# One sum row per token in DRAM instead of four expert rows, in a hybrid decoder layer with 32 experts on Trainium2

## What is computed

```python
x = x + concat([o_da, o_rw]) @ w_out
h = rmsnorm(x, ffn_norm_w)
x = x + moe_ffn(h, ...)          # top 4 of 32 experts per token
return rmsnorm(x, final_norm_w)

# in moe_ffn, per expert block of rows:
gu = xb @ mlp1_w[e] + mlp1_b[e]
act = (up + 1.0) * gate * sigmoid(1.702 * gate)      # clamped gate and up
y = (act @ mlp2_w[e] + mlp2_b[e]) * row_gate
out = zeros((T + 1, D)).at[row_tok].add(y)[:T]
```

## Time and profile before

| | us |
|---|---|
| median of three runs | 1646.55 |
| the three runs | 1646.4, 1647.76, 1646.55 |
| the profiled execution | 1647.25 |
| its span, first to last instruction | 1645.4 |
| TensorE busy | 1574.4 (96%) |
| VectorE busy | 1347.0 (82%) |
| ScalarE busy | 1069.3 (65%) |
| GpSimd busy | 320.8 (19%) |

### The profile page before, as it was taken

The page is one execution under the profiler, slowest core; times in us unless marked ns, Lnnn a source line. Parts: engine busy times, 40 slices in busy tenths (PEclk is TensorE's granted clock), DMA queues, the critical chain, the costliest instruction groups (busy, mean ns, idle before and its releaser), DMA issues.

```text
span 1645.4 us, 28008 instructions
## 1 busy us (share of the span) xinstructions
PE 1574.4 (96%) x10337; PEld 1271.1 (77%) x10338; DVE 1347.0 (82%) x1188; ACT 1069.3 (65%) x1011; POOL 320.8 (19%) x223
## 2 busy tenths in 40 slices
PE   5999999987899999999999999999999999999994
PEld 4677777765778888888888888888888888888883
DVE  5556565556489999999999999999999999999984
ACT  4534343434367777777777777777777777777772
POOL 6300000000102212222121222312222232212222
PEclk9999999998899999999999999999999999999997
DMA  6611111006299999999999999999999999999899
GB/s 194 248 49 32 49 32 47 2 2 221 105 389 350 384 354 367 356 369 357 373 376 361 377 356 365 371 367 360 366 360 348 366 366 362 365 366 366 348 323 210
DMA packets 100718, 467.26 MB, mean 284 GB/s; under 512 B 12696, under 2 KB 39352, under 8 KB 51377
## 3 DMA queue, kind: packets, MB, share of 16 engines
q1 hardware_dynamic: 86032, 429.65, 68.7%
q0 software_dynamic: 14624, 36.74, 7.2%
HBM read 454.84 MB, written 28.31 MB: 294 GB/s over the span
## 4 chain that ended last, share of the span: by engine, by line
PE 71%; DMA 3%; DVE 1%; issue 1%; ACT 0%; PEld 0%; POOL 0%; DVEq 0%; ACTq 0%; POOLq 0%; PEldq 0%
PE psum L1888 29%; PE psum L1891 14%; PE psum L1916 13%; PE psum L1921 6%; PE psum L1294 3%; DMA x<-expert_rows 2%; PE psum L1878 2%; PE psum L1868 2%; PE psum L1904 1%; PE psum L1858 1%; DMA xg<-h_rows,gath_i 0%; DVE w_pieces_lo L1697 0%; PE psum L1310 0%; ACT w_pieces_hi L1562 0%; PE psum L1302 0%
## 5 line engine op out<-in xcount | busy, mean ns | idle before, releaser
L1697 DVE TENSOR_TENSOR w_pieces_lo<-w_pieces,w_pieces_hi 128x2048 fp32r<-128x2048 f32 x384 | 871.0, 2288 | 78.4 <-ACT w_pieces_hi L1562 78.4
L1562 ACT ACTIVATE w_pieces_hi<-w_pieces 128x2048 fp32r<-128x2048 f32 x384 | 736.4, 1919 | 279.3 <-PE psum L1891 204.9
L1888 PE MATMUL psum<-w_pieces_hi,xh 128*128 128x512 f32 x1024 | 292.4, 407 | 0.5 <-DVE xl L1708 0.5
L1888 PE MATMUL psum<-w_pieces_hi,xl 128*128 128x512 f32 x1024 | 276.0, 391 | 0.0
L1891 PE MATMUL psum<-w_pieces_lo,xh 128*128 128x512 f32 x1024 | 275.7, 391 | 0.0
L1888 PEld LDWEIGHTS psum<-w_pieces_hi,xl 128*128 128x128 f32 x1024 | 192.8, 188 | 43.1
L1891 PEld LDWEIGHTS psum<-w_pieces_lo,xh 128*128 128x128 f32 x1024 | 192.3, 188 | 42.7
L1888 PEld LDWEIGHTS psum<-w_pieces_hi,xh 128*128 128x128 f32 x1024 | 181.7, 190 | 41.8 <-issue 11.8
L1516 POOL DMA_INDIRECT expert_rows<-ys,this_i x30 | 158.8, 5294 | 246.5 <-issue 246.5
L1916 PE MATMUL psum<-w_pieces_hi,ah 128*128 128x512 f32 x512 | 160.8, 395 | 0.0
L1916 PE MATMUL psum<-w_pieces_hi,al 128*128 128x512 f32 x512 | 158.2, 390 | 0.0
(11 more groups left out here) (363 smaller groups left out, 1938.7 us busy)
## 6 DMA issues: line engine op xcount, KB each, us to landing
w_pieces<-in_mlp_w SPq DMA_DIRECT2D x384, 1024.0 KB, 6.9
w_raw<-in_w_in SPq DMA_DIRECT2D x26, 512.0 KB, 4.0
expert_rows<-o_t POOLq DMA_DIRECT2D x4, 2048.0 KB, 14.3
x<-expert_rows POOLq DMA_DIRECT2D x16, 512.0 KB, 9.4
w_pieces<-in_w_out SPq DMA_DIRECT2D x8, 512.0 KB, 9.2
chunk_work<-in_x SPq DMA_DIRECT2D x4, 512.0 KB, 5.9
x<-in_x SPq DMA_DIRECT2D x4, 512.0 KB, 13.7
h_rows<-w_pieces POOLq DMA_DIRECT2D x4, 512.0 KB, 3.0
```

Of the source, the lines that this page charges most:

```text
L1562: nc.scalar.activation(hi[:, p % RING], raw[:, raw_slot(b, p)].rearrange("p r n -> p (r n)"), ACT.Copy).then_inc(s_hi, 1)
L1697: nc.vector.tensor_tensor(lo[:, p % RING], raw[:, raw_slot(b, p)].rearrange("p r n -> p (r n)"), hi[:, p % RING].bitcast(F32), ALU.subtrac ...
L1888: nc.tensor.matmul(bank(up_bank(b) + c), a[:, k, :], hi[:, p % RING, c * 512:(c + 1) * 512], start=False, stop=False)
```

## The change

`y_dram` with four rows a token becomes `sum_dram` (shown as sum_rows) with 512 + 128 rows, one a token and 128 spare ones. In the routing GpSimd stores each tile of x (the input plus the mixers' output) there as soon as it is summed, and tile 0 once more into the spare rows; the wait for these stores stands before the first gather. Each expert's scatter now adds to the rows in DRAM. An empty slot, whose token number reads 4096, is sent to spare row 512 + p by taking the smaller of the two numbers, so no row is dropped: all 128 slots are written. At the end four plain loads bring the sums into `x`. The zeros written in the front, the scan and two other small VectorE operations, the constant table `firsts` and the second column of `info` go.

```diff
-        nc.gpsimd.memset(blank, 0.0).then_inc(s_blank, 1)
-        pool.wait_ge(s_blank, 1)
-        for n in range(4):
-            nc.gpsimd.dma_start(g["y_dram"][n * S:(n + 1) * S, :].rearrange("(a p) n -> p a n", p=P),
-                                blank.rearrange("p (a n) -> p a n", a=1).to_broadcast([P, S // P, D])).then_inc(s_blanked, 16)
-        pool.wait_ge(s_blanked, 64)
...
+            pool.wait_ge(s_x2, t + 1)
+            nc.gpsimd.dma_start(g["sum_dram"][t * P:(t + 1) * P, :], x[:, t, :]).then_inc(g["s_kept"], 16)
+            if not t:
+                nc.gpsimd.dma_start(g["sum_dram"][S:S + P, :], x[:, t, :]).then_inc(g["s_kept"], 16)
             pool.wait_ge(s_h2, t + 1)
             nc.gpsimd.dma_start(g["h2_dram"][t * P:(t + 1) * P, :], h2[:, t, :]).then_inc(s_store, 16)
...
-        chain(nc.vector.tensor_scalar(r1[:, 12:16], con("token"), 4.0, -BIG - 1.0, ALU.mult, ALU.add))
...
-        chain(nc.vector.tensor_tensor_scan(which[:].rearrange("p t e -> p (t e)"), con("firsts"), mask.rearrange("p t e -> p (t e)"),
-                                           0.0, ALU.mult, ALU.add))
-        nc.vector.tensor_tensor(info[:, :, 0:EXPERTS, 1], which[:], r1[:, 12:16].rearrange("p (t a) -> p t a", a=1).to_broadcast([P, NT, EXPERTS]),
-                                ALU.add)
...
         pool.wait_ge(s_z, 1)
+        pool.wait_ge(g["s_kept"], 16 * (NT + 1))
...
         def prepare(r, e):
             pool.sem_inc(s_part, 1)
-            nc.gpsimd.tensor_copy(this_i[:], tab[:, bass.ds(e, 1), 1:2].rearrange("p a c -> p (a c)"))
-            nc.gpsimd.tensor_copy(this_g[:], tab[:, bass.ds(e, 1), 2:3].rearrange("p a c -> p (a c)")).then_inc(s_this, 1)
+            nc.gpsimd.tensor_copy(this_f[:], tab[:, bass.ds(e, 1), 0:1].rearrange("p a c -> p (a c)")).then_inc(s_float, 1)
+            nc.gpsimd.tensor_copy(this_g[:], tab[:, bass.ds(e, 1), 2:3].rearrange("p a c -> p (a c)"))
+            pool.wait_ge(s_float, r * SCATTERED + (e + 1))
+            pool.sem_inc(s_part, 1)
+            nc.gpsimd.tensor_scalar(this_i[:], this_f[:], con("spare"), None, ALU.min).then_inc(s_this, 1)
...
-            nc.gpsimd.indirect_dma_start(g["y_dram"], bass.IndirectOffsetOnAxis(this_i[:, 0:1], 0), ys[:], None,
-                                         bounds_check=4 * S - 1, oob_is_err=False).then_inc(s_scat, 16)
+            nc.gpsimd.indirect_dma_start(sum_dram, bass.IndirectOffsetOnAxis(this_i[:, 0:1], 0), ys[:], None,
+                                         compute_op=ALU.add).then_inc(s_scat, 16)
...
-            for k in range(4):
-                for t in LAST_ROWS:
-                    if k:
-                        pool.wait_ge(s_row[t], (r * 4 + k) * 16)
-                        pool.sem_inc(s_part, 1)
-                    nc.gpsimd.dma_start(x[:, t, :], rows_v[t, :, k, :], accum_op=ALU.add).then_inc(s_row[t], 16)
+            for t in LAST_ROWS:
+                nc.gpsimd.dma_start(x[:, t, :], sum_v[t]).then_inc(s_row[t], 16)
...
-                dve.wait_ge(s_row[t], r * 64 + 64)
+                dve.wait_ge(s_row[t], r * 16 + 16)
```

More of the change, by code:

```diff
@@ L88, in constant_tables @@
         "token": np.arange(NT)[None, :] * P + p,
+        "spare": S + p,
         "experts": np.broadcast_to(np.arange(EXPERTS)[None, :], (P, EXPERTS)),
@@ L153, in build_program @@
         h2_dram = nc.dram_tensor("h2_rows", (S, D), F32, kind="Internal").ap()
-        y_dram = nc.dram_tensor("expert_rows", (4 * S, D), F32, kind="Internal").ap()
+        sum_dram = nc.dram_tensor("sum_rows", (S + P, D), F32, kind="Internal").ap()
         rank = sb(top, "rank", [P, NT, INDEXED])
@@ L160, in build_program @@
         with ExitStack() as st:
-            front(nc, d, sb, sem, st, dict(cst=cst, cols=cols, stat=stat, o_t=o_t, y_dram=y_dram), con, ident, psum, bank)
+            front(nc, d, sb, sem, st, dict(cst=cst, cols=cols, stat=stat, o_t=o_t), con, ident, psum, bank)
         x = sb(top, "x", [P, NT, D])
@@ L168, in build_program @@
             s_raw, s_gath = [sem(f"piece_loaded{p}") for p in range(RAW)], sem("rows_gathered")
-            g = dict(x=x, stat=stat, o_t=o_t, rank=rank, info=info, flags=flags, h2_dram=h2_dram, y_dram=y_dram,
+            g = dict(x=x, stat=stat, o_t=o_t, rank=rank, info=info, flags=flags, h2_dram=h2_dram, sum_dram=sum_dram, s_kept=sem("x2_kept"),
                      raw=raw, bias=bias, down_b=down_b, turned=turned, s_raw=s_raw, s_gath=s_gath, s_gates_copied=sem("gates_turned_copied"))
@@ L1091, in output_and_route @@
     hidden = carve(P, NT, EXPERTS)
-    which = carve(P, NT, EXPERTS)
     eg = carve(P, NT, EXPERTS)
@@ L1382, in experts @@
     rank, info, flags, raw, bias, s_raw = (g[k] for k in ("rank", "info", "flags", "raw", "bias", "s_raw"))
-    x, stat, o_t, y_dram, down_b, turned = (g[k] for k in ("x", "stat", "o_t", "y_dram", "down_b", "turned"))
+    x, stat, o_t, sum_dram, down_b, turned = (g[k] for k in ("x", "stat", "o_t", "sum_dram", "down_b", "turned"))
     hi = sb(st, "w_pieces_hi", [P, RING, 2 * D], F32R)
@@ L1400, in experts @@
     this_g = sb(st, "this_g", [P, 1])
+    this_f = sb(st, "this_f", [P, 1])
+    s_float = sem("row_numbers_copied")
     s_hi, s_lo, s_used = sem("piece_hi"), sem("piece_lo"), sem("piece_used")
@@ L1411, in experts @@
     s_blank = sem("gates_blanked")
-    s_row = [sem(f"rows_added{t}") for t in range(NT)]
+    s_row = [sem(f"sums_loaded{t}") for t in range(NT)]
     s_fw, s_add, s_ss, s_sd, s_rs, s_o, s_out = (sem(n) for n in ("final_w_loaded", "sums_ready", "x3_squared", "x3_deviation", "x3_rstd",
                                                                   "out_ready", "out_stored"))
-    s_sel31, s_wiped = sem("last_selected"), sem("expert_rows_wiped")
+    s_sel31, s_wiped = sem("last_selected"), sem("sums_kept_again")
     sel_t = [xh[:, 4 * n:4 * n + 4, :].rearrange("p a b -> p (a b)") for n in range(2)]
@@ L1420, in experts @@
     gate_last = [tab[:, e, 2:3] for e in (EXPERTS - 2, EXPERTS - 1)]
-    rows_v = y_dram.rearrange("(t p k) n -> t p k n", p=P, k=4)
+    sum_v = sum_dram[0:S].rearrange("(t p) n -> t p n", p=P)
     last_banks = {0: 6, 3: 2, 1: 0, 2: 4}
@@ L1544, in again @@
             pool.sem_inc(s_part, 1)
-            for n in range(4):
-                nc.gpsimd.dma_start(y_dram[n * S:(n + 1) * S, :].rearrange("(a p) n -> p a n", p=P),
-                                    xg[:].rearrange("p (a n) -> p a n", a=1).to_broadcast([P, S // P, D])).then_inc(s_wiped, 16)
+            for t in range(NT):
+                nc.gpsimd.dma_start(sum_v[t], x[:, t, :]).then_inc(s_wiped, 16)
             pool.wait_ge(s_wiped, r * 64)
```

7 lines of the change are left out of this document (1 added, 6 removed).

## The result

| | before | changed |
|---|---|---|
| median, us | 1646.86 (6 runs, 1646.12 to 1647.76) | 1636.25 (6 runs, 1635.65 to 1637.17) |
| the profiled execution, us | 1647.25 | 1635.65 |
| its span, us | 1645.4 | 1633.9 |
| mean granted clock | 0.983 | 0.986 |

The ratio is 0.9934, with a 95% interval from 0.9924 to 0.9943: 10.6 us faster. The forecast was 1636.0. A second series of the same kernel gave 1636.35 against 1647.14 (0.9934, 0.9921 to 0.9948).

What follows compares the result with a forecast made beforehand. TensorE was taken to bound the expert loop and sixteen accumulating loads the tail; 1647.25 us less 10.7 gave 1636.6, and with the profiled execution 0.7 above the median, 1635.9, say 1636.0 us, range 1634 to 1642.

Steps and rivals of the forecast that it cites:

- The tail: Kernel's end: four plain loads replace sixteen adding ones, third final addition at 1623.27 instead of 1633.98, 10.7 us gained.
- The loads hidden: Tail: the four plain loads land at about 1600 to 1609, before 1618.39, under the last two experts' down projections.
- The addition into DRAM: Loop scatters: adding 128 rows costs what its reads cost, 2.5 us of all sixteen engines; ends 1.3 and 7.5.
- Added to the loop: Expert loop: new scatter's 2.5 us less the old one's 0.65 adds 1.85 us of DMA time; path cost 0.
- The room in the loop: Expert loop: 13.1 MB at 408 GB/s needs 32.2 of the 36.05 us period, so 3.9 us are spare.
- The burst: Loop weight loads: 2.5 us more makes 10.4 us at most, under the tightest slot's 11.6; +5 us in all kept.
- Rival 1: Expert loop gets ragged, the tightest slot met late: 0.15 us for each of 30 experts, 1640.5; chance 0.08.
- the ring: Six slots in which the loop's weight pieces turn round; the tightest freed slot is needed 11.6 us later.
- Rival 2: Weight conversions in every expert: additions starve the weight stream, from 4.5 us a scatter; 1687 at 6.2 us; chance 0.08.
- Rival 3: Expert loop: memory, at most 364 GB/s, is the limit, every added byte paid, 2.2 us x 30, 1701; chance 0.03.
- Rival 4: Tail does not move, loads or something unseen still ending it; loads would need 28 us; 1646.5; chance 0.02.
- The front and the routing: Before the loop: zeros gone, five x stores added before the first gather; cost 0, upper bound 3.5 us, gain 0.

Runs made afterwards that it cites:

- the tripled run: Changed kernel with every scatter made three times, back to back, the extra two adding into DRAM tensors nobody reads: 1718.71 us, ratio 1.044.
- The doubled scatter: Changed kernel with every scatter made twice, the second adding into a DRAM tensor nobody reads, its landing waited for: 1636.13 us, ratio 0.993.
- the undone tail: Changed kernel with its four plain final loads replaced by sixteen adding loads in four rounds with the old waits: 1647.39 us against 1647.47.

## Why the prediction was right, point by point

- **The tail, 10.7 us.** 10.65 measured from the last scatter on. The first addition was forecast at 1619.07 and stands at 1618.22; with the 0.85 us by which everything lay earlier in this execution, at 1619.07. The third was forecast at 1623.27 and stands, so counted, at 1623.31. The new stall in front of the reciprocal was forecast at 0.3 us and is 0.41. Since place, cause and size agree, the total of 1636.0 against 1636.25 is not luck.
- **The loads hidden.** Right, with 8.1 us to landing against the 7.3 assumed from the earlier trace rows, issued by 1591.05, needed at 1618.2. One reading on the way was off without harm: the transfer that ends at 1601.30 in the earlier trace rows is that of the second tile of the round, whose next load is issued at 1601.84; the first tile's had landed by 1599.36.
- **The addition into DRAM, 2.5 us of the engines.** Right: 2.64 us. That it costs twice the plain rows' 1.28 fits the argument from its reads (8 KB for a row of 4 KB), but no run took the reads apart.
- **Added to the loop, 1.85 us an expert.** The queue's share rose by 5.5% of 36.05 us, 1.98 us.
- **The room in the loop, 3.9 us.** Mis-sized, though the forecast did not hang on it, since the cost was nothing either way. The prediction let the scatter take up to 4.5 us before the loop slows; 5.3 us were still free of charge, and the estimate of the edge is 5.2. It took 408 GB/s, the best 10 us of the front, as the ceiling of a stream of 1 MB pieces. Turned round, the tripled run gives the ceiling that was there: 12 pieces of 1.049 MB in 38.8 - 7.9 - 0.7 = 30.2 us, which is 417 GB/s (an estimate, since busy shares that add up to 1.02 cannot be taken off the period exactly).
- **The burst.** Forecast: a load at most 10.4 us against a tightest need at 11.6. The landing's maximum rose from 9.3 to 11.6 us in 560 to 1560 us, 1.2 more than forecast, so the margin that the prediction worked out was used up, and still no conversion waited on a load; the middle rose from 6.9 to 7.7.
- **Rival 1, a ragged loop.** The period did not move. The doubled scatter shows that the ring forgives even 36 late pieces.
- **Rival 2, starving.** The mechanism is real and stands in the tripled run, with the place and the sign that were named. One added scatter, 2.64 us, uses half of the room of about 5.2 us. The sign alone, a load in front of a conversion, was too early a warning, as the doubled run shows.
- **Rival 3, a memory limit at 364 GB/s.** The changed loop moves 371 GB/s and the doubled one 386 with TensorE still full. A limit of about 358 GB/s for one core, which the Trainium skill states (page DMA: Bandwidth & Descriptors, section Where 436 GB/s comes from), does not show in this case, where one core runs alone.
- **Rival 4, a tail that does not move.** The loads would have had to take 28 us; they took 8.1, and the tail moved.
- **The front and the routing, nothing.** Right: zeros put back cost nothing, and the five stores end before they are waited for. The last store of x is issued at 437.18 and the last h2 store at 441.49. The first gather is at 449.06 instead of 448.44, so the sign that the prediction gave for a cost came true by 0.6 us. The stores are not its cause: the first `sel`, which waits for no store, already comes 0.62 us later (445.65 against 445.03). Nor was it a cost: the gather has landed at 453.26 against 454.04.

## What to carry to other kernels

A DMA that adds cost its engines about twice a plain one of the same size here (2.64 against 1.28 us for the scatter, 2.5 to 2.65 against about 1.5 for the loads), so a row of them at the end of a kernel, with less work beside them than they take, is the worst place; spread over this loop, with DMA time to spare, they were free. Where such room is in question, double and triple the suspected load: the DMA share stood at 1.02 both where it cost nothing and where it cost 82 us. When a wait is removed, read what is late next and order that work by who needs it first; here this gave 2.3 to 2.5 us more.

## What the runs showed of the hardware that was not expected

**The clock in the routing.** In the changed kernel's profile the granted TensorE clock fell earlier than in the one before. The stretch 438 to 442 us reads, before and after:

```profile
438.00:442.00 4.00, 3.23 (x28) 3.01 (x27) 3.16 (x11) 2.91 (x6) 0.00 (x0) 1.00 0.00 0
```

```profile
438.00:442.00 4.00, 3.90 (x23) 3.79 (x22) 2.65 (x9) 2.33 (x5) 0.51 (x1) 0.62 0.32 131
```

1.00 (2.4 GHz) against 0.62, a mean on the way to 0.50 (1.2 GHz). TensorE had just worked on the projection in both, without a gap from 400 to 435 us, and both had a granted clock of 1.00 at 436 to 438 us. With the fall 22 small products of the router took 4.34 us instead of 2.82:

```profile
438.50 2.82 PE L1310 MATMUL psum<-rw_scaled,w_pieces 128*128 128x32 f32 x22
```

```profile
437.93 4.34 PE L1297 MATMUL psum<-rw_scaled,w_pieces 128*128 128x32 f32 x22
```

So the first gather came 0.6 us later although the projection had ended 0.58 us earlier. From the last sum to the first `sel` (L1679 before) it took 8.8 us before and 10.0 after, and 10.0 in the second profile of the changed kernel too. But the other profiles spread as widely with either routing: 8.4 and 9.6 in the two kernels with the old one, 8.4 to 10.0 in those with the new one, 8.45 of them in the undone tail, where the clock stayed at 1.00 to 445 us. The earlier fall is thus no fixed part of the change; whether the change makes it more frequent stays open. It did not delay the first gather's data either: between 17.3 and 17.8 us after the start of the last sum the first gather has landed in all thirteen, whether the clock fell early or late.

**Landing of an added scatter** is nearly the same with 64 of its 128 rows in bounds as with all of them (15.3 and 15.5 us), and 2 us above a plain one.
